# Query projection of a two-layer decoder trunk: sets of 256 columns and all tokens become sets of 512 columns and half of the tokens

## The chip, the core and the metric

The kernel is one program on one core of a Trainium2 chip. A core has five engines with an instruction stream each: TensorE (PE; matrix products from SBUF into the eight PSUM banks, 512 float32 per partition and bank), VectorE (DVE), ScalarE (ACT), GpSimd (POOL), and SyncE (SP), which here only issues DMAs. They run in parallel and meet at semaphores. The metric is the device time of one execution in microseconds (us), the median of several runs.

## What is computed

A gMLP layer with its feed-forward network, keys and values shared by what follows, then an attention layer with its own feed-forward network; 1,024 tokens, width 1,024, everything float32. The change lies in the queries of the attention layer:

```python
def swa_sink_attention(x, k_band, v_band, g_norm, w_q, g_q, sinks, w_o):
    q = (rms_norm(x, g_norm) @ w_q).reshape(b, s, N_Q_HEADS, HEAD_DIM)      # 1024 x 1024 @ 1024 x 1024, 16 heads of 64
    q = rms_norm(q, g_q).reshape(b, nb, BLOCK, N_KV_HEADS, Q_PER_KV, HEAD_DIM)
    logits = jnp.einsum("bntkgd,bnskd->bnkgts", q, k_band)
    ...
```

and just ahead of it, in `shared_kv`, the keys and values: `rms_norm(x, g_kv) @ w_kv` (1,024 x 512), the keys normalised per head as well.

## The kernel before

**Three products for one.** Each float32 operand is split into an upper part (hi, a copy rounded to the type that TensorE reads, made by ScalarE) and the rest (lo, a subtraction by VectorE). `three` issues hi x hi, hi x lo and lo x hi into the same bank.

**Columns.** Between the first feed-forward network and attention, TensorE computes key columns, query columns and value columns. The token tiles (128 tokens; parts `h_hi_b`, `h_lo_b`, one tensor per half of the tokens) are the stationary side, the weights the moving side. `columns(s, ...)` makes one set: 256 output columns for all 8 token tiles, 8 tiles of the inner dimension k, in 4 banks (`4 * s` and up: set 1 writes banks 4 to 7, set 0 banks 0 to 3). First the keys (set 0), then four query sets with s = 1, 0, 1, 0, then the value columns. Sets take turns on the two groups of banks: `cols_free[s]` says that VectorE has read a group, `cols_full[s]` that a set is complete, `cols_half` that the first 4 k are done for all tokens.

**Weights.** A set's weights are two tiles of 128 x 1,024 (4 k x 256 columns each, 512 KB), one for each of two slots. SP loads a tile into `w_raw[slot]` once the tile before it in this slot has been split (`w_ready`), GpSimd multiplies it by the gain of the norm (`gains`, signals `w_scaled`), ScalarE copies the upper part to `w_hi[slot]` (`split_scaled`, signals `w_hi_done`), VectorE subtracts into `w_lo[slot]` (`split`, signals `w_ready`). ScalarE must leave `w_hi[0]` alone until `cols_half`, and `w_hi[1]` until `cols_full`.

**Normalisation.** The token factors come from two matmuls with one column (`mean(2, 0)`, `mean(2, 1)`), which TensorE puts between the key matmuls and which write into banks 6 and 7. VectorE reads each with `mean_square` and signals `rec_done`. Ahead of the first query set TensorE waits for `rec_done` at 6, that is for both. After each set, ScalarE squares the 2,048 elements in PSUM (`head_squares`), VectorE sums them by head, ScalarE takes the root (`head_root`), VectorE refines it and multiplies the set out of PSUM into `q_sb` or `k_sb` (`head_norm`), which frees the banks.

**The order is written out by hand**, engine by engine. TensorE transposes the normalised keys (`keys_first`, into banks 4 and 5) inside the fourth query set, beside entry `(0, 4)`: after 4 k of the fifth token tile. It waits there for the set before to have left banks 4 to 7.

In the code below, `banks` is PSUM, `link` makes VectorE wait for its own last instruction, and `beside` maps a place in a set to something that is issued there.

Of the kernel before, what the change touches and what calls it, by code (L numbers as in the profile page):

```python
# [6 lines left out]
P = 128  # L7
# [3 lines left out]
NCH = T // P  # L11
# [172 lines left out]
def build(nc, x_t, w_av, w_au, w_ao, w_f_in, w_f_out, w_kv, w_q, w_o, w_s, b_s, params, c_dram, x_dram, out_t):  # L184
    ctx = ExitStack()
    with ctx:
        def sem(name):
            return ctx.enter_context(nc.semaphore(name))
# [91 lines left out]
        q_sb = sb("q_sb", [P, NKV, NCH, QPK * HD], F32)  # L280
        k_sb = sb("k_sb", [P, NCH, NKV * HD], F32)
        vv_sb = sb("vv_sb", [P, NCH, NKV * HD], F32)
        kdup = sb("kdup", [P, NCH, 2, HD], F32)
# [24 lines left out]
        dv_lo_first = sb("dv_lo_first", [P, STRIPS, HD], F32R)  # L308
        dv_raw_first = sb("dv_raw_first", [P, STRIPS, HD], F32, plan[0] - 4 * STRIPS * HD)

        def p_of(block):
# [90 lines left out]
        w_ready = [sem(f"w_ready{s}") for s in range(RING)]  # L402
        cols_half = sem("cols_half")
        x_landed = [[sem(f"x_landed{half}_{k}") for k in range(4)] for half in range(2)]
        w_scaled = [sem(f"w_scaled{s}") for s in range(2)]
# [318 lines left out]
        def _(pool):  # L724
# [106 lines left out]
            last.then_inc(consts_done, 1)  # L831
            with pool.Fori(0, 4) as i:
                for c in use:
                    c.enter(i, 1)
                gains(COL_B_NORM)
                for c in use:
                    c.leave(4)
            gains(COL_KV_NORM)
# [103 lines left out]
        def _(act):  # L942
# [73 lines left out]
            for k in (KT - 2, KT - 1):  # L1016
# [3 lines left out]
                                 ACT.Copy).then_inc(ws_hi_done, 1)  # L1020

            def split_pair(s, split):

                act.wait_ge(cols_half, halves.add())
                split(0)
                act.wait_ge(cols_full[s], cols[s].add())
                split(1)

# [347 lines left out]
            def head_root():  # L1376
                act.wait_ge(hms_done, heads.add())
                nc.scalar.activation(small[:, 2, :], small[:, 3, :], ACT.Sqrt).then_inc(hroot, 1)

            act.wait_ge(cols_half, halves.add())  # L1380
            split_scaled(0)
            root(2, 0)
            act.wait_ge(cols_full[0], cols[0].add())
            split_scaled(1)
            root(2, 1)
# [11 lines left out]

            def q_columns(s):
                split_pair(s, split_scaled)
                head_squares(s)  # L1400
                head_root()
# [96 lines left out]

            q_columns(1)
            q_columns(0)  # L1500
            act.wait_ge(cols_free[1], 2 + COLS_A)
            k_twice(0)
            q_upper(0, 0)
            q_columns(1)
            act.wait_ge(consts_done, 8)
            biases(0)
            act.wait_ge(gain_ready, 1)
            keys_upper(4)
            q_columns(0)
            nc.scalar.preload_act_table(ACT.Exp)  # L1510
# [49 lines left out]
        def _(dve):  # L1560
# [585 lines left out]

            def head_norm(s, dst):

                n = heads.add()
                dve.wait_ge(hsq_done, n)  # L2150
                link(nc.vector.tensor_reduce(small[:, 1, :],
                                             nrm[:, 0:2, :].rearrange("p a (h d) -> p (a h) d", d=HD),
                                             AX_X, ALU.add))
                link(nc.vector.tensor_tensor(by_token(small[:, 1, :]), by_token(small[:, 1, :]), r_square, ALU.mult))
                link(nc.vector.tensor_scalar(small[:, 1, :], small[:, 1, :], EPS, None, ALU.add))
                nc.vector.reciprocal(small[:, 3, :], small[:, 1, :]).then_inc(hms_done, 1)
                dve.wait_ge(hroot, n)
                refine(small[:, 2, :], small[:, 2, :], small[:, 1, :], small[:, 3, :])
                link(nc.vector.tensor_tensor(by_token(small[:, 2, :]), by_token(small[:, 2, :]), r_token, ALU.mult))
                nc.vector.tensor_tensor(dst, flat(4 * s, 4).rearrange("p (h d) -> p h d", d=HD),  # L2160
                                        small[:, 2, :].unsqueeze(2).broadcast_to([P, NCH * QPK, HD]),
                                        ALU.mult).then_inc(cols_free[s], 1)
# [5 lines left out]
            r_square = small[:, 0, NCH:2 * NCH].unsqueeze(2).broadcast_to([P, NCH, NKV])  # L2168
            split(0)
            mean_square(2, 0)  # L2170
            token_root(2, 0, 0)
            mean_square(2, 1)
            split(1)
            token_root(2, 1, 0)
# [14 lines left out]

            def q_columns(s, j):  # L2190
                split(0)
                split(1)
                head_norm(s, q_sb[:, j, :, :].rearrange("p n (h d) -> p (n h) d", d=HD))

# [73 lines left out]

            q_columns(1, 0)
            q_columns(0, 1)  # L2270
            q_columns(1, 2)
            keys_lower(4)
            q_columns(0, 3)
            for j in range(NKV):
# [48 lines left out]
        def _(pe):  # L2323
# [485 lines left out]

            columns(1, h_hi_b, h_lo_b)  # L2810
            columns(0, h_hi_b, h_lo_b)
            columns(1, h_hi_b, h_lo_b)
            columns(0, h_hi_b, h_lo_b, None, {(0, 4): keys_first})
            pe.wait_ge(cols_free[1], cols[1].now())
# [92 lines left out]
```

## Time and profile before

| | |
|---|---|
| median of 3 runs | 1923.89 us (1923.83 to 1926.9) |
| the profiled execution | 1924.28 us, its span 1922.6 us |
| TensorE busy | 1899.4 us, 99% |
| VectorE busy | 1455.1 us, 76% |
| ScalarE busy | 890.9 us, 46% |
| GpSimd busy | 471.0 us, 24% |
| bytes by DMA | 199.08 MB, 104 GB/s in the mean |

The span runs from the first to the last instruction of the profiled execution. Matmuls are pipelined, so one row's duration overlaps the next row's; the distance between starts is what a matmul costs. The four query sets lie between 960 and 1053 us. In the answers of the trace, PE is TensorE, DVE VectorE, ACT ScalarE, POOL GpSimd, L with a number is a line of the code above, and x with a number is a count of instructions.

### The profile page before, as it was taken

The page shows a single profiled execution, that of the slowest core. Times are in us where ns is not written, and L with a number is a line of the kernel's source. Part 1 is how long each engine was busy: PE and PEld are TensorE (multiplying, and loading weights), DVE is VectorE, ACT ScalarE, POOL GpSimd, SP SyncE. Part 2 cuts the span into 40 slices and gives each one's busy share as a digit, 9 for nine tenths or more (in the row PEclk, how much of TensorE's full clock was granted, in tenths as well). Part 3 has the DMA queues.
Part 4 walks back from the last instruction along what each step waited for, and adds up shares of the span by engine and source line. Part 5 has one row for each costly group of instructions (what it writes and reads, how often), then busy time and mean ns, then how long its engine had stood idle before and what let it go on. Part 6 is the DMA issues. An engine that isn't in the chain of part 4 may idle for free.

```text
span 1922.6 us, 27830 instructions
## 1 busy us (share of the span) xinstructions
PE 1899.4 (99%) x9784; PEld 1625.6 (85%) x9784; DVE 1455.1 (76%) x2116; ACT 890.9 (46%) x1575; POOL 471.0 (24%) x408
## 2 busy tenths in 40 slices
PE   8999999999999999999999999999999999999999
PEld 8988888878888888888999988878788888888887
DVE  6366758988878876887854677789978887877875
ACT  6242534544444444444522666656444444444443
POOL 0000001333333320011111566651423333301010
PEclk9999999999999999999999999999999999999999
DMA  5111243122212239963111010040222221279681
GB/s 180 45 44 44 88 131 110 66 88 87 87 65 87 87 125 318 294 152 69 34 45 46 11 56 23 12 154 22 100 76 87 87 87 65 97 247 309 180 169 66
DMA packets 63402, 199.08 MB, mean 104 GB/s; under 512 B 5200, under 2 KB 5584, under 8 KB 56144
## 3 DMA queue, kind: packets, MB, share of 16 engines
q1 hardware_dynamic: 48656, 163.29, 24.3%
q0 software_dynamic: 14656, 34.61, 8.3%
q8 instruction: 55, 0.90, 0.2%
q14 instruction: 35, 0.29, 0.0%
HBM read 162.22 MB, written 35.65 MB: 103 GB/s over the span
## 4 chain that ended last, share of the span: by engine, by line
PE 93%; DVE 4%; issue 1%; ACT 1%; DMA 1%; POOL 0%; ACTq 0%; SPq 0%; DVEq 0%
PE banks L2356 29%; PE banks L2358 29%; PE banks L2357 29%; PE banks L2727 2%; DVE xT L1895 1%; PE banks L2705 1%; PE banks L2706 1%; PE banks L2692 1%; DVE xT L1902 1%; PE banks L2753 1%; DVE fw_lo L1853 1%; PE banks L2478 1%; PE banks L2338 0%; DMA b<-c_scratch 0%; DVE xT L1911 0%
## 5 line engine op out<-in xcount | busy, mean ns | idle before, releaser
L2356 PE MATMUL banks<-t_hi,fw_hi 128*128 128x512 f32 x1248 | 487.8, 391 | 5.9 <-issue 1.5
L2358 PE MATMUL banks<-t_hi,fw_lo 128*128 128x512 f32 x1248 | 486.1, 389 | 0.0
L2357 PE MATMUL banks<-t_lo,fw_hi 128*128 128x512 f32 x1216 | 473.6, 389 | 0.0
L2356 PEld LDWEIGHTS banks<-t_hi,fw_hi 128*128 128x128 f32 x1248 | 234.4, 188 | 59.3 <-issue 3.3
L2358 PEld LDWEIGHTS banks<-t_hi,fw_lo 128*128 128x128 f32 x1248 | 234.4, 188 | 48.5
L2357 PEld LDWEIGHTS banks<-t_lo,fw_hi 128*128 128x128 f32 x1216 | 228.4, 188 | 46.8
L752 POOL TENSOR_TENSOR nrm<-raw 128x512 f32<-128x512 f32 x40 | 55.8, 1394 | 721.5 <-DVE fw_lo L1853 428.3
L2356 PE MATMUL banks<-fw_hi,fw_hi 128*128 128x512 f32 x544 | 212.0, 390 | 0.9 <-DVE fw_lo L2012 0.9
L2358 PE MATMUL banks<-fw_hi,fw_lo 128*128 128x512 f32 x544 | 211.9, 389 | 0.0
L2357 PE MATMUL banks<-fw_lo,fw_hi 128*128 128x512 f32 x544 | 211.8, 389 | 0.0
L1299 ACT ACTIVATE fw_hi<-b 128x512 fp32r<-128x512 f32 x154 | 97.1, 631 | 227.0 <-PE banks L2358 215.4
L1214 ACT ACTIVATE xT<-xT,par 128x1024 f32<-128x1024 f32 x88 | 109.3, 1245 | 165.8 <-DVE xT L1881 108.4
L2012 DVE TENSOR_TENSOR fw_lo<-b,fw_hi 128x512 fp32r<-128x512 f32 x154 | 106.4, 691 | 104.7 <-ACT fw_hi L1299 104.6
L1895 DVE SCALAR_TENSOR_TENSOR xT<-xT,par 128x1023 f32<-128x1023 f32 x88 | 150.2, 1707 | 0.0
L1853 DVE TENSOR_TENSOR fw_lo<-raw,fw_hi 128x512 fp32r<-128x512 f32 x120 | 122.4, 1020 | 17.9 <-ACT fw_hi L1188 17.9
L1188 ACT ACTIVATE fw_hi<-nrm 128x512 fp32r<-128x512 f32 x160 | 99.6, 626 | 64.4 <-PE banks L2358 64.4
L1853 DVE TENSOR_TENSOR fw_lo<-nrm,fw_hi 128x512 fp32r<-128x512 f32 x160 | 113.2, 710 | 18.6 <-ACT fw_hi L1188 15.4
L1572 DVE TENSOR_TENSOR w_lo<-w_raw,w_hi 128x1024 fp32r<-128x1024 f32 x43 | 56.8, 1323 | 85.5 <-ACT w_hi L953 43.2
L2356 PEld LDWEIGHTS banks<-fw_hi,fw_hi 128*128 128x128 f32 x544 | 102.2, 188 | 22.7 <-issue 1.8
L2357 PEld LDWEIGHTS banks<-fw_lo,fw_hi 128*128 128x128 f32 x544 | 102.2, 188 | 21.2
L2358 PEld LDWEIGHTS banks<-fw_hi,fw_lo 128*128 128x128 f32 x544 | 102.2, 188 | 21.1
L1902 DVE SCALAR_TENSOR_TENSOR xT<-xT,par 128x1022 f32<-128x1022 f32 x88 | 115.7, 1315 | 0.2
(240 smaller groups left out, 4104.4 us busy)
## 6 DMA issues: line engine op xcount, KB each, us to landing
raw<-in_w_f_in SPq DMA_DIRECT2D x44, 1024.0 KB, 5.0
c_scratch<-xT SPq DMA_DIRECT2D x44, 512.0 KB, 2.6
b<-c_scratch SPq DMA_DIRECT2D x16, 1024.0 KB, 9.5
a_sum<-in_w_f_out POOLq DMA_DIRECT2D x16, 1024.0 KB, 14.5
raw<-in_w_f_out SPq DMA_DIRECT2D x54, 256.0 KB, 11.1
w_raw<-in_w_ao SPq DMA_DIRECT2D x16, 512.0 KB, 3.7
x_scratch<-xT SPq DMA_DIRECT2D x4, 2048.0 KB, 7.9
xT<-x_scratch SPq DMA_DIRECT2D x8, 1024.0 KB, 17.5
```

The costliest lines, as they stand in the source:

```text
L752: nc.gpsimd.tensor_tensor(w_sum(0), a21, a22, ALU.add).then_inc(sums_done, 1)
L1188: nc.scalar.activation(fw_hi[n % RING_F], weight(q, source), ACT.Copy).then_inc(fw_hi_done, 1)
L1214: nc.scalar.activation(y_row(q, r), z_row(q, r), ACT.Identity, bias=par[:, bass.ds(tile + (conv + 6 * FT), 1)], scale=par[:, bass.ds(tile ...
L1299: nc.scalar.activation(tok_hi[n % 3], out_token(n), ACT.Copy).then_inc(c_hi_done, 1)
L1572: nc.vector.tensor_tensor(w_lo[:, slot, :], src[:, slot, :], w_hi[:, slot, :].bitcast(F32), ALU.subtract).then_inc(w_ready[slot], 1)
L1853: nc.vector.tensor_tensor(fw_lo[n % RING_F], weight(q, PRODUCTS[p][0]), fw_hi[n % RING_F].bitcast(F32), ALU.subtract).then_inc(fw_ready, 1)
L1895: link(nc.vector.scalar_tensor_tensor(out=y[:, 1:T], in0=z[:, 0:T - 1], scalar=par[:, bass.ds(i * 2 + (q * FT + r + conv + 2 * FT), 1)], i ...
L1902: nc.vector.scalar_tensor_tensor(out=y[:, 2:T], in0=z[:, 0:T - 2], scalar=par[:, bass.ds(i * 2 + (q * FT + r + conv), 1)], in1=y[:, 2:T], ...
L2012: nc.vector.tensor_tensor(tok_lo[n % 3], out_token(n), tok_hi[n % 3].bitcast(F32), ALU.subtract).then_inc(c_ready, 1)
L2356: nc.tensor.matmul(out, w_h, m_h, start=start, stop=False, **kw)
L2357: nc.tensor.matmul(out, w_h, m_l, start=False, stop=False, **kw)
L2358: return nc.tensor.matmul(out, w_l, m_h, start=False, stop=stop, **kw)
```

## The change

A query set becomes 512 columns for half of the tokens: 4 token tiles, one bank each. `wide_columns(s, pair, half, order, beside)` issues it; the four sets are (columns 0 to 511, first half), (the same columns, second half), and the two for columns 512 to 1,023. The weights of a pair of sets are four pieces of two k x 512 columns (`by_wide` lays them out so), and a piece serves both halves. Four split pieces must stay at hand, so two more places are made, `q_2` over `raw_1` and `q_3` over `vv_sb`, which the values fill later; the raw slots remain two. Pieces 0 and 1 go to `q_2` and `q_3`, pieces 2 and 3 to the old slots 0 and 1, pieces 4 to 7 to slots 0 and 1, `q_2`, `q_3`. `piece_free` counts pieces that a second half is through with. Two heads' groups (j) come out of one set, so the last multiply is two instructions. The value weights' splits go behind `piece_free` 4 and 5.

```diff
+        vv_at = plan[0]
...
+        q_2 = sb("q_2", [P, 2, HB], F32R, raw_1_at)
+        q_3 = sb("q_3", [P, 2, HB], F32R, vv_at)
+        q_slots = [(w_hi[:, 0, :], w_lo[:, 0, :]), (w_hi[:, 1, :], w_lo[:, 1, :]),
+                   (q_2[:, 0, :], q_2[:, 1, :]), (q_3[:, 0, :], q_3[:, 1, :])]
+
+        def q_slot(piece):
+
+            pair, m = piece // 4, piece % 4
+            return q_slots[(m + 2 * (1 - pair)) % 4]
...
-            with pool.Fori(0, 4) as i:
-                for c in use:
-                    c.enter(i, 1)
-                gains(COL_B_NORM)
-                for c in use:
-                    c.leave(4)
+            for piece in range(8):
+                s, k = piece % 2, COL_B_NORM + 2 * (piece % 4)
+                w = w_raw[:, s, :].rearrange("p (k c) -> p k c", k=2)
+                pool.wait_ge(w_landed[s], use[s].add() * 16)
+                nc.gpsimd.tensor_tensor(w, w, par[:, k:k + 2].unsqueeze(2).broadcast_to([P, 2, 512]),
+                                        ALU.mult).then_inc(w_scaled[s], 1)
...
+            def wide_upper(piece):
+
+                slot = piece % 2
+                act.wait_ge(w_scaled[slot], use[slot].add() - LOADS_BEFORE_KV)
+                nc.scalar.activation(q_slot(piece)[0], w_raw[:, slot, :], ACT.Copy).then_inc(w_hi_done[slot], 1)
+
+            wide_upper(0)
+            wide_upper(1)
             act.wait_ge(cols_half, halves.add())
-            split_scaled(0)
+            wide_upper(2)
             root(2, 0)
             act.wait_ge(cols_full[0], cols[0].add())
-            split_scaled(1)
+            wide_upper(3)
             root(2, 1)
             head_squares(0)
             head_root()
...
-            def q_columns(s):
-                split_pair(s, split_scaled)
+            def q_norm(s):
+                act.wait_ge(cols_full[s], cols[s].add())
                 head_squares(s)
                 head_root()
...
-            q_columns(1)
-            q_columns(0)
+            q_norm(1)
+            for piece in (4, 5, 6):
+                act.wait_ge(piece_free, piece - 3)
+                wide_upper(piece)
+            q_norm(0)
+            wide_upper(7)
             act.wait_ge(cols_free[1], 2 + COLS_A)
             k_twice(0)
             q_upper(0, 0)
-            q_columns(1)
+            q_norm(1)
             act.wait_ge(consts_done, 8)
             biases(0)
             act.wait_ge(gain_ready, 1)
             keys_upper(4)
-            q_columns(0)
+            for s in range(2):
+                act.wait_ge(piece_free, 3 + s + 1)
+                split_scaled(s)
+            q_norm(0)
             nc.scalar.preload_act_table(ACT.Exp)
             biases(1)
             q_copy(1, 2)
...
+            def wide_lower(piece):
+
+                slot, (hi, lo) = piece % 2, q_slot(piece)
+                dve.wait_ge(w_hi_done[slot], use[slot].add())
+                nc.vector.tensor_tensor(lo, w_raw[:, slot, :], hi.bitcast(F32), ALU.subtract).then_inc(w_ready[slot], 1)
+
+            wide_lower(0)
             mean_square(2, 0)
+            wide_lower(1)
+            wide_lower(2)
             token_root(2, 0, 0)
             mean_square(2, 1)
-            split(1)
+            wide_lower(3)
             token_root(2, 1, 0)
...
+            def q_norm(s, pair, half):
+
+                n = slice(4 * half, 4 * half + 4)
+                head_factors(lambda row: row.rearrange("p (n h) -> p n h", h=2 * QPK),
+                             *(small[:, 0, t].unsqueeze(2).broadcast_to([P, 4, 2 * QPK])
+                               for t in (slice(NCH + 4 * half, NCH + 4 * half + 4), n)))
+                whole = flat(4 * s, 4).rearrange("p (n j h d) -> p n j h d", n=4, j=2, h=QPK)
+                factor = small[:, 2, :].rearrange("p (n j h) -> p n j h", n=4, j=2)
+                for j in range(2):
+                    last = nc.vector.tensor_tensor(
+                        q_sb[:, 2 * pair + j, n, :].rearrange("p n (h d) -> p n h d", d=HD), whole[:, :, j, :, :],
+                        factor[:, :, j, :].unsqueeze(3).broadcast_to([P, 4, QPK, HD]), ALU.mult)
+                last.then_inc(cols_free[s], 1)
...
-            q_columns(1, 0)
-            q_columns(0, 1)
-            q_columns(1, 2)
+            q_norm(1, 0, 0)
+            for piece in (4, 5, 6):
+                wide_lower(piece)
+            q_norm(0, 0, 1)
+            wide_lower(7)
+            q_norm(1, 1, 0)
             keys_lower(4)
-            q_columns(0, 3)
+            split(0)
+            split(1)
+            q_norm(0, 1, 1)
...
-            columns(1, h_hi_b, h_lo_b)
-            columns(0, h_hi_b, h_lo_b)
-            columns(1, h_hi_b, h_lo_b)
-            columns(0, h_hi_b, h_lo_b, None, {(0, 4): keys_first})
+            def wide_columns(s, pair, half, order, beside=None):
+
+                pe.wait_ge(cols_free[s], cols[s].now())
+                for m in order:
+                    hi, lo = q_slot(4 * pair + m)
+                    if half == 0:
+                        pe.wait_ge(w_ready[m % 2], use[m % 2].add())
+                    for n in range(4):
+                        for k in (2 * m, 2 * m + 1):
+                            c, t = slice(k % 2 * 512, (k % 2 + 1) * 512), slice(n * P, (n + 1) * P)
+                            mm = three(banks[:, 4 * s + n, :], h_hi_b[half][:, k, t], h_lo_b[half][:, k, t],
+                                       hi[:, c], lo[:, c], k == 2 * order[0], k == 2 * order[-1] + 1,
+                                       skip_group_check=True)
+                    if m == order[-1]:
+                        mm.then_inc(cols_full[s], 1)
+                    elif half:
+                        mm.then_inc(piece_free, 1)
+                    if beside is not None and m == order[0]:
+                        beside()
+                cols[s].add()
+
+            wide_columns(1, 0, 0, (0, 1, 2, 3))
+            wide_columns(0, 0, 1, (2, 3, 0, 1))
+            wide_columns(1, 1, 0, (0, 1, 2, 3))
+            wide_columns(0, 1, 1, (0, 1, 2, 3), keys_first)
...
+    def by_wide(w):
+        return w.reshape(4, 2, P, 2, 512).transpose(3, 0, 2, 1, 4).reshape(-1, P, HB)
...
-        "w_q": by_columns(a["b_w_q"][0]),
+        "w_q": by_wide(a["b_w_q"][0]),
```

`head_norm` is cut in two in the change: `head_factors`, which takes the rows of factors as arguments, and the multiply. The hunks stand in this order: tiles, GpSimd, ScalarE, VectorE, TensorE, layout of the weights.

In the built program, VectorE's stretch that begins with the adding up of the squares of norm 2 (`nrm`), before; `small` holds the factors, L1596 with L1598 is a mean's read:

```order
L1589 TENSOR_TENSOR nrm_54<-nrm_54 128x512 [waits sq_added,sq_done] x13
L1572 TENSOR_TENSOR w_lo_61<-w_raw_55,w_hi_60 128x1024 [waits w_hi_done0]
L1596 TENSOR_SCALAR small_53<-banks 128x4 [waits ms_full]
L1598 RECIPROCAL small_53<-small_53 128x4 [waits dve_step]
L1577 TENSOR_TENSOR small_53<-small_53 128x4 [waits root_done]
L1578 SCALAR_TENSOR_TENSOR small_53<-small_53 128x4 [waits dve_step]
L1580 SCALAR_TENSOR_TENSOR small_53<-small_53 128x4 [waits dve_step]
L1596 TENSOR_SCALAR small_53<-banks 128x4 [waits ms_full,dve_step]
L1598 RECIPROCAL small_53<-small_53 128x4 [waits dve_step]
L1572 TENSOR_TENSOR w_lo_61<-w_raw_55,w_hi_60 128x1024 [waits w_hi_done1]
```

The same place in the changed kernel; L2198 is `wide_lower`, L1616 with L1618 a mean's read:

```order
L1609 TENSOR_TENSOR nrm_54<-nrm_54 128x512 [waits sq_added,sq_done] x13
L2198 TENSOR_TENSOR q_2_139<-w_raw_55,q_2_139 128x1024 [waits w_hi_done0]
L1616 TENSOR_SCALAR small_53<-banks 128x4 [waits ms_full]
L1618 RECIPROCAL small_53<-small_53 128x4 [waits dve_step]
L2198 TENSOR_TENSOR q_3_140<-w_raw_55,q_3_140 128x1024 [waits w_hi_done1]
L2198 TENSOR_TENSOR w_lo_61<-w_raw_55,w_hi_60 128x1024 [waits w_hi_done0]
L1597 TENSOR_TENSOR small_53<-small_53 128x4 [waits root_done]
L1598 SCALAR_TENSOR_TENSOR small_53<-small_53 128x4 [waits dve_step]
L1600 SCALAR_TENSOR_TENSOR small_53<-small_53 128x4 [waits dve_step]
L1616 TENSOR_SCALAR small_53<-banks 128x4 [waits ms_full,dve_step]
L1618 RECIPROCAL small_53<-small_53 128x4 [waits dve_step]
```

The second read of a mean stood behind one split and the first token root; it now stands behind three splits and that root, and the third of the three is that of piece 2, the second to wait for `w_hi_done0`.

ScalarE at the same place, before (L953 is a weight split, L966 a root of a token mean):

```order
L953 ACTIVATE w_hi_60<-w_raw_55 128x1024 [waits w_scaled0,cols_half]
L966 ACTIVATE small_53<-small_53 128x4 [waits rec_done]
L953 ACTIVATE w_hi_60<-w_raw_55 128x1024 [waits w_scaled1,cols_full0]
L966 ACTIVATE small_53<-small_53 128x4 [waits rec_done]
L1373 ACTIVATE nrm_54<-banks 128x2048
```

and in the changed kernel (L1389 is `wide_upper`):

```order
L1389 ACTIVATE q_2_139<-w_raw_55 128x1024 [waits w_scaled0]
L1389 ACTIVATE q_3_140<-w_raw_55 128x1024 [waits w_scaled1]
L1389 ACTIVATE w_hi_60<-w_raw_55 128x1024 [waits w_scaled0,cols_half]
L978 ACTIVATE small_53<-small_53 128x4 [waits rec_done]
L1389 ACTIVATE w_hi_60<-w_raw_55 128x1024 [waits w_scaled1,cols_full0]
L978 ACTIVATE small_53<-small_53 128x4 [waits rec_done]
L1378 ACTIVATE nrm_54<-banks 128x2048
```

Two copies came in front of the one that waits for `cols_half`, and that one's tile is now the third of the query weights.

TensorE in the fourth query set, around the key transposes (`kdup`), before, where they follow 108 matmuls of their set:

```order
L2357 MATMUL banks<-w_lo,h_hi_b_106 128x256
L2358 MATMUL banks<-w_hi,h_lo_b_108 128x256
L2774 MATMUL banks<-ident,kdup 128x128 [waits kdup_done,cols_free1,consts_done]
L2774 MATMUL banks<-ident,kdup 128x128 x7
L2356 MATMUL banks<-w_hi,h_hi_b_106 128x256
```

and in the changed kernel, where they follow 24 of 96:

```order
L2404 MATMUL banks<-w_lo,h_hi_b_106 128x512
L2405 MATMUL banks<-w_hi,h_lo_b_108 128x512
L2821 MATMUL banks<-ident,kdup 128x128 [waits kdup_done,cols_free1,consts_done]
L2821 MATMUL banks<-ident,kdup 128x128 x7
L2403 MATMUL banks<-w_hi,h_hi_b_106 128x512
```

The transposes and what they wait for are the same; fewer matmuls, twice as wide, stand in front of them.

## Rows read from the trace of the kernel before

**Rows 1.** The page: span, and each engine's busy time.
```profile
span 1922.6 us, 27830 instructions
...
PE 1899.4 (99%) x9784; PEld 1625.6 (85%) x9784; DVE 1455.1 (76%) x2116; ACT 890.9 (46%) x1575; POOL 471.0 (24%) x408
```

**Rows 2.** The page: chain that ended last, shares by engine.
```profile
PE 93%; DVE 4%; issue 1%; ACT 1%; DMA 1%; POOL 0%; ACTq 0%; SPq 0%; DVEq 0%
```

**Rows 3.** Busy time by window; columns named in the first row.
```profile
core 0: us, PE busy (x) PEld busy (x) DVE busy (x) ACT busy (x) POOL busy (x), PEclk, DMA share, GB/s
...
sum 93.00, PE 93.00 PEld 93.00 DVE 46.76 ACT 20.09 POOL 15.86; mean PE 18.60 PEld 18.60 DVE 9.35 ACT 4.02 POOL 3.17
```

**Rows 4.** Timeline, TensorE, first query set: start us, duration us, what.
```profile
960.11 0.28 PE L2358 MATMUL banks<-w_hi,h_lo_b 128*128 128x256 f32 x1
...
982.91 0.28 PE L2356 MATMUL banks<-w_hi,h_hi_b 128*128 128x256 f32 x1
```

**Rows 5.** Timeline, TensorE, last FFN matmuls, 512 columns.
```profile
923.63 0.39 PE L2358 MATMUL banks<-fw_hi,tail_lo 128*128 128x512 f32 x1
...
935.19 0.39 PE L2358 MATMUL banks<-fw_hi,tail_lo 128*128 128x512 f32 x1
```

**Rows 6.** Timeline, ScalarE: splits (L953), squares (L1373).
```profile
960.43 1.06 ACT L953 ACTIVATE w_hi<-w_raw 128x1024 fp32r<-128x1024 f32 x1 [2.72 <-PE banks L2358]
...
1054.41 1.86 ACT L1373 ACTIVATE nrm<-banks 128x2048 f32<-128x2048 f32 x1
```

**Rows 7.** Timeline, VectorE: splits (L1572), means read (L1596, L1598).
```profile
955.96 1.23 DVE L1572 TENSOR_TENSOR w_lo<-w_raw,w_hi 128x1024 fp32r<-128x1024 f32 x1
...
957.29 0.18 DVE L1598 RECIPROCAL small<-small 128x4 f32<-128x4 f32 x1
...
958.34 0.16 DVE L1596 TENSOR_SCALAR small<-banks 128x4 f32<-128x4 f32 x1
958.53 0.18 DVE L1598 RECIPROCAL small<-small 128x4 f32<-128x4 f32 x1
961.52 2.45 DVE L1572 TENSOR_TENSOR w_lo<-w_raw,w_hi 128x1024 fp32r<-128x1024 f32 x1 [2.81 <-ACT w_hi L953]
963.89 0.15 DVE L1577 TENSOR_TENSOR small<-small 128x4 f32<-128x4 f32 x1
```

**Rows 8.** Timeline, GpSimd: scaling of query weights after their load.
```profile
960.99 1.89 POOL L815 TENSOR_TENSOR w_raw<-w_raw,par 128x1024 f32<-128x1024 f32 x1 [18.43 <-DMA w_raw<-in_w_q]
967.87 1.89 POOL L815 TENSOR_TENSOR w_raw<-w_raw,par 128x1024 f32<-128x1024 f32 x1 [4.99 <-DMA w_raw<-in_w_q]
```

**Rows 9.** Timeline, TensorE, at the program's start.
```profile
6.13 0.55 PE L2356 MATMUL banks<-w_hi,h_hi_a 128*128 128x256 f32 x1 [6.13 <-DVE w_lo L1661]
...
10.53 0.42 PE L2358 MATMUL banks<-w_hi,h_lo_a 128*128 128x256 f32 x1
10.74 0.36 PE L2356 MATMUL banks<-w_hi,h_hi_a 128*128 128x256 f32 x1
```

**Rows 10.** Busy time, granted clock (column PEclk) of two of those microseconds.
```profile
8.00:10.00 2.00, 2.00 (x11) 2.00 (x11) 0.39 (x2) 0.85 (x2) 0.00 (x0) 1.00 0.97 356
```

**Rows 11.** Waits of TensorE: us in total, times, longest us.
```profile
PE banks L2356 <- DVE w_lo L1661: 6.1, 1, 6.1
...
PE banks L2338 <- DVE nrm L1589: 1.0, 1, 1.0
```

**Rows 12.** Timeline, VectorE: last multiply of a normalisation (L2160), values (L2227).
```profile
1038.56 2.29 DVE L2160 TENSOR_TENSOR q_sb<-banks,small 128x2048 f32<-128x2048 f32 x1
...
1060.63 2.29 DVE L2160 TENSOR_TENSOR q_sb<-banks,small 128x2048 f32<-128x2048 f32 x1
...
1068.14 1.22 DVE L2227 TENSOR_TENSOR vv_sb<-banks,small 128x1024 f32<-128x1024 f32 x1
```

**Rows 13.** Timeline, TensorE: key transposes (L2774), query transposes (L2692).
```profile
1042.31 1.04 PE L2774 MATMUL banks<-ident,kdup 128*128 128x128 f32 x8
...
1063.33 0.60 PE L2692 MATMUL banks<-ident,q 128*128 128x128 f32 x4
```

More of the change, by code:

```diff
@@ L403, in build @@
         cols_half = sem("cols_half")
+        piece_free = sem("piece_free")
         x_landed = [[sem(f"x_landed{half}_{k}") for k in range(4)] for half in range(2)]
@@ L1020, in _ @@
                                  ACT.Copy).then_inc(ws_hi_done, 1)
[L1022 to L1026, printed above, removed]
-                split(1)
             def rows_keep(half):
@@ L2145, in _, with head_factors @@
             heads = Count()
-            def head_norm(s, dst):
+            def head_factors(by_token, r_square, r_token):
                 n = heads.add()
@@ L2159, in head_norm @@
                 link(nc.vector.tensor_tensor(by_token(small[:, 2, :]), by_token(small[:, 2, :]), r_token, ALU.mult))
+            def head_norm(s, dst):
+                head_factors(by_token, r_square, r_token)
                 nc.vector.tensor_tensor(dst, flat(4 * s, 4).rearrange("p (h d) -> p h d", d=HD),
@@ L2168, in _ @@
             r_square = small[:, 0, NCH:2 * NCH].unsqueeze(2).broadcast_to([P, NCH, NKV])
-            split(0)
+            def wide_lower(piece):
[3 more added lines that the diff above has]
+            wide_lower(0)
             mean_square(2, 0)
+            wide_lower(1)
+            wide_lower(2)
             token_root(2, 0, 0)
             mean_square(2, 1)
-            split(1)
+            wide_lower(3)
             token_root(2, 1, 0)
@@ L2188, in _ @@
             dve.wait_ge(gain_ready, 1)
[L2190 to L2193, printed above, removed]
+            def q_norm(s, pair, half):
[10 more added lines that the diff above has]
+                last.then_inc(cols_free[s], 1)
             sums = small[:, 7, 0:4]
```

## The prediction

> **What bounds the kernel now.** Read the shares first: TensorE is busy for 1899.4 of 1922.6 us, VectorE for 76% [rows 1], and the chain that ended last is 93% TensorE [rows 2]. So time is saved only where TensorE issues less, and lost wherever it stands. Then read the stretch that the change rewrites, the four sets of query columns: from 960 to 1053 us TensorE is busy for all 93.00 us [rows 3], so each set follows the last without a gap and no wait ends late here. ScalarE, VectorE and GpSimd together have work for less than that, and their waits in this stretch are cover, not cost. That cover is what the change spends.
>
> The unit is the start-to-start pace of TensorE, not the "busy" of a row, which overlaps its neighbours. With 256 columns, 191 matmuls start between 960.11 and 982.91: 22.80 / 190 = 0.1200 us [rows 4]. With 512 columns, 52 start between 923.63 and 935.19: 11.56 / 51 = 0.2267 us [rows 5]. Two narrow ones cost 0.2400, one wide one 0.2267: a matmul has about 13.3 ns that do not depend on its width.
>
> **Part 1, fewer matmuls: -5.1 us.** Each set was 8 tiles of tokens x 8 k x 3 products = 192 narrow matmuls, four sets 768: 768 x 0.1200 = 92.2 us. Now it is 4 tiles x 8 k x 3 = 96 wide ones, four sets 384: 384 x 0.2267 = 87.0 us. All of it is on the path. The Trainium skill (TensorE: Matmul & The Clock Gate, Back-to-back issue gap) gives an isolated matmul its columns over 2.4 GHz plus 2.5 ns; by that the 384 matmuls saved would be worth only 1.0 us, and the sum below would come out 4.1 us higher. This trace has both widths side by side and shows 13.3 ns, so I go by the rows and give that rule no chance of its own.
>
> The bytes, loads, scalings by GpSimd (8 of 1.9 us), splits by ScalarE and VectorE (8 each of 1.06 and about 1.2 us) stay eight each. What moves is their order and what each waits for. The final multiply of a normalisation becomes two of 1,024 elements in place of one of 2,048 (2.29 us [rows 12]). The nearest 1,024-element one took 1.22 us [rows 12], so 2.44 against 2.29: +0.15 us on VectorE, to be counted where somebody waits for it.
>
> **Part 2, the start of the first set: +6.6 us.** TensorE may not open the first query set, which writes banks 4 to 7, before the two token means have been read out of banks 6 and 7 (it waits for rec_done at 6). In the kernel before, the second of these two reads stood behind one split only and ended at 958.71 [rows 7], 1.5 us before the key columns finished: ScalarE's copy, released by their last matmul, starts at 960.43 [rows 6], and a matmul lasts 0.28 us [rows 4] with some 0.05 for the signal, so the last began at 960.1 and the next set at 960.2. The wait was hidden. Now VectorE has wide_lower(1) and wide_lower(2) between the first read and the second, as the rows of the order show. Piece 2 is the third to use raw slot 0 here, and can't be early:
> - wide_lower(0) ends as the old split did, 955.96 + 1.23 = 957.19 [rows 7], and only then may SP load piece 2 into slot 0. GpSimd started on the load that this very moment released at 960.99 and took 1.89 us: scaled at 962.88 [rows 8]. The same here.
> - ScalarE's upper part takes 1.06 us [rows 6]: 963.97.
> - wide_lower(1) follows the first mean's read (957.47) and takes 1.23: 958.7. Its slot's load reaches GpSimd 3.8 to 3.9 us after such a split, as 957.19 to 960.99 and 963.97 to 967.87 [rows 7, 8], so at about 962.6. GpSimd is free at 962.88 and is busy with piece 3 until 964.77.
> - VectorE's subtraction started at 961.52 and took 2.45 us in place of 1.23, ending 1.09 us after GpSimd's end at 962.88 [rows 7, 8]: beside a running GpSimd multiply it makes hardly any way. So wide_lower(2) ends 1.09 us after 964.77, at 965.9, not at 965.2.
> - Three small operations of the root (the first at 963.89, each some 0.2 after the one before) and the two of the mean (958.34 to 958.71, 0.37) [rows 7]: about 0.9 us more. rec_done reaches 6 at 966.75, TensorE starts at 966.8 instead of 960.2: 6.6 us. Without the overlap on VectorE it would be 5.9; both stay in the range.
>
> What is next late after that stall? Piece 3 is ready by 968, and is needed 16 us into the set (3 x 24 x 0.2267). Nothing.
>
> **Part 3, the clock behind that stall: +2.0 us.** Where TensorE stood for 6.1 us, at the program's start [rows 11], its first 21 matmuls of 256 columns, from 6.13 up to the start of the next at 10.74 us, had a pace of some 0.21 us [rows 9], against the 0.12 of [rows 4]. The profile's granted clock reads 1.00 even there [rows 10], but 256 columns in 0.213 us are 1.2 GHz, the lower level. The 21 took 4.61 us where 21 x 0.12 = 2.52 would have done: 2.1 us lost. A stand of 6.4 us (6.6 less the last matmul's run) is as long as that one, and no other wait of TensorE is over 1.0 us [rows 11], so this is the nearest row; I take 2.0 us, with 0 as the other end, since a start from rest need not equal a pause in full work. The same page of the Trainium skill (Why this matters for your kernels) warns against idle gaps between bursts of matmuls for this reason; by it the clock falls here, and denied, the sum is 2.0 us lower.
>
> **Part 4, the key transposes: +3.4 us.** keys_first waits until the set before it has left banks 4 to 7 (cols_free[1]). It stood behind 108 of the fourth set's 192 matmuls, 13.0 us in, and the transposes at 1042.31 [rows 13] came after the normalisation's end (1038.56 + 2.29 = 1040.85 [rows 12]) with 1.4 us to spare. Now it stands behind the first of four pieces: 24 x 0.2267 = 5.4 us in. What it waits for got shorter, but not that short: ScalarE's squares begin some 0.2 us after the set before has issued its last matmul, and from the squares' start at 1054.41 [rows 6] to the end of the last multiply (1060.63 + 2.29 = 1062.92 [rows 12]) are 8.5 us with no GpSimd multiply in it. 0.2 + 8.5 + 0.15 for the second multiply + 0.05 for the signal = 8.9 us; 8.9 - 5.4 = 3.5, and I take 3.4. GpSimd has by then scaled all ten loads, so nothing stretches it. Queued behind this wait on TensorE are the other 72 matmuls of the set and all of the value columns. At the low end, if the squares start at once, it is 3.2.
>
> **What stays covered.** The third set needs piece 7 at 16.3 us. Its raw tile waits for the end of set two, then ScalarE does squares, root and split, VectorE the whole normalisation (8.9 us) and 1.2 us of split: 10 to 11 us. 5 us to spare. Pieces 4 to 6 are released 5.4, 10.9 and 16.3 us into set two; VectorE is through its normalisation at 8.9 us, and the last of the three is split by 16.3 + 1.06 + 1.2 = 18.6 us, before that set ends at 21.8. SP's loads keep their order and their condition (the split of the tile before in the same slot); each waits in its raw slot, scaled, for its release. The value weights are split during the last set (their releases come at its first and second piece, ScalarE passes its key copy about 1 us after the transposes), 8 us before their use. After the last set the query transposes come 84 x 0.12 = 10.1 us in and need a normalisation of 8.9: hidden, as before (1063.33 [rows 13] against 1062.92).
>
> **The sum.** -5.1 + 6.6 + 2.0 + 3.4 = +6.9 us. The profiled execution took 1924.28 us with a span of 1922.6; the median of the three runs is 1923.89, 0.4 below it. I put the sum on the median: 1930.8 us.
>
> **Rivals.**
> - The clock does not fall: -5.1 + 6.6 + 3.4 = +4.9, 1928.8 us. For it: a pause may not be treated as a cold start, and no row shows a clock lost in mid-program. Against: the stand is as long as the one row there is. With the unblocked VectorE it is +4.0, 1927.9.
> - The clock falls in both stands: +9 us, 1932.9. The second stand is half as long as the row that shows it; small.
> - Only one stand occurs, since I have misread one of the two waits. Only the first: -5.1 + 6.6 = +1.5 (or +3.5 with the clock), 1925.4 to 1927.4; only the second: -1.7, 1922.2.
> - Faster: the first stand isn't there because rec_done is not behind piece 2. It would be so if the means' read reached VectorE ahead of wide_lower(2), and the key transposes' wait were over in 5.4 us. Then only the saving stands, 1918.8 us. It decides at the place of one VectorE instruction: the read must be over by 960.2, and piece 2 alone isn't scaled before 962.88. The order speaks against it.
>
> **How the numbers follow.** Forecast 0.62; no clock loss 0.18; one stand only 0.10; no stand 0.07; clock lost twice 0.03. A measurement of this kernel can tell about 0.2% (3.8 us) from no change. Slower by more is the forecast, the double loss and most of the second case (+4.9 is close to the bound: 0.13 of 0.18): 0.78. Within: the rest of it and one stand only, 0.15. Faster: 0.07. The range goes from the unblocked no-clock case with some scatter, 1927.5, to the double loss, 1933.0; outside it lie one stand only, no stand, and a little more: under 2 in 10.
>
> **What would show it.** In the profile after: 384 matmuls of 512 columns with pace 0.227 in this stretch; one TensorE wait of over 6 us released by VectorE's reciprocal of the mean, in front of the first wide matmul; behind it 512-column matmuls at some 0.43 us for about 4 us (part 3), or at 0.227 at once (its rival); one wait of some 3.4 us in front of the eight key transposes. The forecast is wrong if the first wait is under 4 us, if wide matmuls keep another pace, or if a third wait shows up at a set's start.

## The result: 1935.03 us, slower by 10.6 us, and the profile after

| | before | after |
|---|---|---|
| median | 1924.41 us (1923.83 to 1926.9, 5 runs) | 1935.03 us (1934.4 to 1936.73, 5 runs) |
| ratio | | 1.0052, 95% interval 1.004 to 1.0064 |
| span of the profiled execution | 1922.6 us | 1933.3 us |

The way was forecast, the size was not: 1930.8 us was predicted, with a range up to 1933.0. The change is 0.55% of the kernel, small but outside the interval of the ratio. Three of the five runs before are the ones that the forecast was added to.

The page of the changed kernel: span, busy time, and the chain's shares by engine.

```profile
span 1933.3 us, 27052 instructions
...
PE 1900.0 (98%) x9400; PEld 1609.1 (83%) x9400; DVE 1446.7 (75%) x2120; ACT 891.5 (46%) x1575; POOL 473.6 (24%) x408
...
PE 89%; DVE 6%; issue 2%; ACT 1%; DMA 1%; POOL 0%; ACTq 0%; SPq 0%; DVEq 0%
```

TensorE issues 384 matmuls less [rows 1], but its share of the chain falls from 93% [rows 2] to 89%, and VectorE's rises to 6%: TensorE is being waited for less, and waits more. What it waits for stands in the view of its waits (us in total, times, longest us).

```profile
PE banks L2403 <- DVE small L1618: 7.0, 1, 7.0
PE banks L2403 <- DVE w_lo L1681: 6.2, 1, 6.2
PE banks L2821 <- issue: 3.3, 1, 3.3
```

The second row is the old one of the program's start [rows 11]. The first and the third are new, and they are the two stands of the prediction: 7.0 us in front of the first wide set, released by VectorE's reciprocal of a mean (L1618), and 3.3 us in front of the key transposes (L2821), where the view names no releaser ("issue").

The first stand, TensorE's timeline (start us, duration us):

```profile
962.66 0.28 PE L2405 MATMUL banks<-w_hi,h_lo_b 128*128 128x256 f32 x1
969.93 0.80 PE L2403 MATMUL banks<-q,h_hi_b 128*128 128x512 f32 x1 [6.99 <-DVE small L1618]
970.52 0.63 PE L2404 MATMUL banks<-q,h_hi_b 128*128 128x512 f32 x1
970.95 0.63 PE L2405 MATMUL banks<-q,h_lo_b 128*128 128x512 f32 x1
...
973.51 0.63 PE L2405 MATMUL banks<-q,h_lo_b 128*128 128x512 f32 x1
...
974.32 0.39 PE L2404 MATMUL banks<-q,h_hi_b 128*128 128x512 f32 x1
974.55 0.40 PE L2405 MATMUL banks<-q,h_lo_b 128*128 128x512 f32 x1
```

The last key matmul starts at 962.66 and the first wide one at 969.93 in place of 962.78: 7.15 us. Ten wide matmuls start from there up to 974.32: the first two 0.59 us apart, the others 0.43; from 974.32 on it is 0.227, as in [rows 5]. VectorE meanwhile:

```profile
958.52 1.23 DVE L2198 TENSOR_TENSOR q<-w_raw,q 128x1024 fp32r<-128x1024 f32 x1
959.66 0.15 DVE L1616 TENSOR_SCALAR small<-banks 128x4 f32<-128x4 f32 x1
959.85 0.18 DVE L1618 RECIPROCAL small<-small 128x4 f32<-128x4 f32 x1
959.94 1.20 DVE L2198 TENSOR_TENSOR q<-w_raw,q 128x1024 fp32r<-128x1024 f32 x1
966.82 2.18 DVE L2198 TENSOR_TENSOR w_lo<-w_raw,w_hi 128x1024 fp32r<-128x1024 f32 x1 [5.68 <-ACT w_hi L1389]
968.92 0.15 DVE L1597 TENSOR_TENSOR small<-small 128x4 f32<-128x4 f32 x1
...
969.50 0.16 DVE L1616 TENSOR_SCALAR small<-banks 128x4 f32<-128x4 f32 x1
969.70 0.18 DVE L1618 RECIPROCAL small<-small 128x4 f32<-128x4 f32 x1
```

wide_lower(0), the first mean's read, wide_lower(1), then nothing until wide_lower(2) at 966.82, and the second mean's read behind it. In the kernel before, that read followed the first by 1.2 us [rows 7]. GpSimd's two multiplies say what wide_lower(2) waited for and why it took 2.18 us:

```profile
963.74 1.89 POOL L848 TENSOR_TENSOR w_raw<-w_raw,par 128x1024 f32<-128x1024 f32 x1 [18.62 <-DMA w_raw<-in_w_q]
966.02 1.89 POOL L848 TENSOR_TENSOR w_raw<-w_raw,par 128x1024 f32<-128x1024 f32 x1 [0.39 <-DMA w_raw<-in_w_q]
```

Piece 2 is scaled at 965.63; piece 3's multiply runs until 967.91, and wide_lower(2) ends 1.09 us after that, as in [rows 7, 8].

The granted clock (PEclk, third from the end of a row) in windows of 2 us, from 966 on and then from 1042 on:

```profile
core 0: us, PE busy (x) PEld busy (x) DVE busy (x) ACT busy (x) POOL busy (x), PEclk, DMA share, GB/s
966.00:968.00 2.00, 0.00 (x0) 0.00 (x0) 1.18 (x1) 0.88 (x2) 1.89 (x1) 0.86 0.00 0
968.00:970.00 2.00, 0.07 (x1) 0.07 (x1) 1.86 (x7) 1.15 (x2) 0.00 (x0) 0.50 0.00 0
...
972.00:974.00 2.00, 2.00 (x7) 1.54 (x6) 2.00 (x1) 0.00 (x0) 1.10 (x1) 0.50 0.73 190
...
1044.00:1046.00 2.00, 0.00 (x0) 0.00 (x0) 2.00 (x2) 0.03 (x1) 0.00 (x0) 0.99 0.00 0
1046.00:1048.00 2.00, 1.75 (x9) 1.78 (x10) 0.15 (x1) 0.00 (x0) 0.00 (x0) 0.50 0.00 0
1048.00:1050.00 2.00, 2.00 (x7) 1.59 (x7) 0.56 (x1) 1.71 (x2) 0.00 (x0) 0.66 0.00 0
1050.00:1052.00 2.00, 2.00 (x10) 1.66 (x9) 1.86 (x2) 0.35 (x1) 0.00 (x0) 1.00 0.00 0
```

It falls to 0.50 (1.2 of 2.4 GHz) while TensorE stands, both times (the second time just ahead of 1046), and is back at 1.00 some 3 to 4.5 us after work has begun again. The second stand:

```profile
1042.58 0.39 PE L2405 MATMUL banks<-w_hi,h_lo_b 128*128 128x512 f32 x1
1046.25 1.94 PE L2821 MATMUL banks<-ident,kdup 128*128 128x128 f32 x8 [3.29 <-issue]
1047.84 0.78 PE L2403 MATMUL banks<-w_hi,h_hi_b 128*128 128x512 f32 x1
1048.42 0.63 PE L2404 MATMUL banks<-w_lo,h_hi_b 128*128 128x512 f32 x1
```

The eight transposes take 1.6 us there, 0.79 in the kernel before ([rows 13], and the next start at 1043.10), and the wide matmuls behind them start at half pace. The view names no releaser, but the last multiply of the normalisation, in two parts now, ends at 1046.15, 0.10 us before they start:

```profile
1043.80 2.35 DVE L2232 TENSOR_TENSOR q_sb<-banks,small 128x1024 f32<-128x1024 f32 x2
```

They also wait for `kdup`, which ScalarE writes from 1022.0 on, in 1.04 us, so it was there long before.

### The profile page after: what moved, and what is told of

It reads as the page before. It is cut to its first block, busy times and chain, and to the rows that moved or that the text cites. A ratio compares the mean times of both kernels' runs of the same rounds, so it can differ in the third digit from the quotient of the medians.

```text
span 1933.3 us, 27052 instructions
## 1 busy us (share of the span) xinstructions
PE 1900.0 (98%) x9400; PEld 1609.1 (83%) x9400; DVE 1446.7 (75%) x2120; ACT 891.5 (46%) x1575; POOL 473.6 (24%) x408
## 4 chain that ended last, share of the span: by engine, by line
PE 89%; DVE 6%; issue 2%; ACT 1%; DMA 1%; POOL 0%; ACTq 0%; SPq 0%; DVEq 0%
PE banks L2403 28%; PE banks L2405 28%; PE banks L2404 28%; PE banks L2774 2%; DVE xT L1915 1%; DVE xT L1922 1%; PE banks L2752 1%; PE banks L2753 1%; PE banks L2739 1%; PE banks L2800 1%; DMA b<-c_scratch 1%; DVE fw_lo L1873 1%; PE banks L2525 1%; DVE nrm L1609 1%; DVE h_lo_b L2145 0%
## 5 line engine op out<-in xcount | busy, mean ns | idle before, releaser
L770 POOL TENSOR_TENSOR nrm<-nrm,raw 128x512 f32<-128x512 f32 x40 | 83.2, 2079 | 75.3 <-DVE fw_lo L1873 75.3
## 6 DMA issues: line engine op xcount, KB each, us to landing
raw<-in_w_f_out SPq DMA_DIRECT2D x54, 256.0 KB, 10.6
```

Of the source, the lines that this page charges most:

```text
L770: nc.gpsimd.tensor_tensor(w_sum(3), w_sum(1), a12, ALU.add).then_inc(sums_done, 1)
```

## A measure with little scatter

By the traces the changed kernel is 10.7 us longer, but 2.55 us of that arise before the changed code is reached: GpSimd's first instruction there, released by the feed-forward network's last matmul, starts at 938.20 and not at 935.65. So this study compares the stretch from that instruction (the MEMSET of wraps) to ScalarE's first copy of the query transposes (qT), which is the same work in every kernel. Before, and then the changed kernel:

```profile
935.65 0.20 POOL L821 MEMSET wraps<- 128x128 f32 x1 [56.05 <-PE banks L2358]
```

```profile
1063.96 0.60 ACT L1410 ACTIVATE qT<-banks 128x512 fp32r<-128x512 f32 x1 [1.68 <-PE banks L2692]
```

```profile
938.20 0.21 POOL L833 MEMSET wraps<- 128x128 f32 x1 [56.76 <-PE banks L2405]
```

```profile
1075.70 0.60 ACT L1423 ACTIVATE qT<-banks 128x512 fp32r<-128x512 f32 x1 [2.62 <-PE banks L2739]
```

128.31 us against 137.50. The table has this stretch for every profile, and the whole kernel's median less that of the kernel before, as run beside it (for the changed kernel's first row: the five runs above). One profile is one execution, so each stretch is a single reading; the two of the kernel before agree to 0.01 us, the two of the changed kernel to 0.24:

| kernel | stretch, us | less 128.31 | whole kernel, us | interval of the ratio |
|---|---|---|---|---|
| before | 128.31 | | | |
| before, again | 128.31 | 0.00 | -0.4 | 0.9989 to 1.001 |
| changed | 137.50 | +9.19 | +10.6 | 1.004 to 1.0064 |
| changed, again | 137.74 | +9.43 | +10.2 | 1.004 to 1.0067 |
| mean read ahead | 128.34 | +0.03 | +1.5 | 1.0 to 1.0018 |
| keys late | 132.24 | +3.93 | +5.4 | 1.0015 to 1.0038 |
| both | 123.28 | -5.03 | -4.4 | 0.9968 to 0.9986 |
| narrow sets, mean read late | 134.57 | +6.26 | +6.4 | 1.0023 to 1.0045 |
| both, a stand of 2 us made | 125.39 | -2.92 | -2.6 | 0.9979 to 0.9997 |
| both, a stand of 1 us made | 124.03 | -4.28 | -3.7 | 0.9969 to 0.9987 |

## The experiments

**The first stand alone.** One step of VectorE's moved back to where it had been in effect, in the changed kernel:

```diff
             mean_square(2, 0)
+            mean_square(2, 1)
             wide_lower(1)
             wide_lower(2)
             token_root(2, 0, 0)
-            mean_square(2, 1)
             wide_lower(3)
```

> The changed kernel with one VectorE step moved: the read of the second token mean stands right behind the first, ahead of wide_lower(1) and wide_lower(2). Theory (the first stand is the wait for that read, behind piece 2's chain): the stand in front of the first wide set, 7.15 us start to start in the profile after, is gone, and with it the 10 matmuls at half pace behind it (2.1 us); the stand at the key transposes stays. 1935.0 - 9.3 = 1925.7 us. Rival (TensorE would next wait for a piece of weights at the same place): the stand shrinks to the time of that piece, and at least 3 us of the 9.3 stay.

Measured: 1926.78 us (1925.18 to 1929.01, 11 runs) beside 1925.29 of the kernel before (25 runs), 9.1 us less than the +10.6 of the changed kernel. In its trace TensorE has no wait there, and the first wide matmul starts at 962.00, with the next at 962.23:

```profile
962.00 0.40 PE L2403 MATMUL banks<-q,h_hi_b 128*128 128x512 f32 x1
962.23 0.40 PE L2404 MATMUL banks<-q,h_hi_b 128*128 128x512 f32 x1
```

The stretch is 9.16 us shorter. The theory holds (it expected 1.3 us over the kernel before, and 1.5 were measured; the total lies 1 us above the expected 1925.7, as the kernel before lay above its 1924.4); no piece of weights was next late.

**The second stand alone.** In `wide_columns`, in the changed kernel:

```diff
-                    if beside is not None and m == order[0]:
+                    if beside is not None and m == order[1]:
```

> The changed kernel with the key transposes of the fourth wide set behind its second piece (10.9 us in) in place of its first (5.4 us). Theory: the normalisation that they wait for ends 8.9 us in, so the second stand (3.5 us) and the half pace behind it (1.5 us) are gone: 1935.0 - 5.0 = 1930.0 us, with the first stand as it was. Rival (the transposes wait for something else, as the profile names no releaser there): no gain.

Measured: 1930.67 us (1929.23 to 1932.7, 7 runs), 5.4 over the kernel before, so 5.2 less than the changed kernel, where 5.0 were expected; in the stretch 5.26 less. The transposes stand without a wait and take 1.04 us again:

```profile
1048.61 1.04 PE L2821 MATMUL banks<-ident,kdup 128*128 128x128 f32 x8
```

So what they waited for was there 10.9 us into the set, and that it was the normalisation is shown by its end: in the two versions below, in which the wait is shorter, the transposes start 0.10 to 0.11 us after the last multiply once more (1035.77 and 1035.88, 1036.78 and 1036.88).

**Both.**

> Both moves. Theory: no stand is left, only the saving of 384 matmuls: 5.1 us under the kernel before, 1924.4 - 5.1 = 1919.3 us. Rival (the wide form costs something outside the four sets too; the profile after was 2.6 us late already at 936 us, ahead of the changed stretch, and had won back 1.0 us by the end): some 1.5 us of it stays, 1920.9 us.

Measured: 1920.89 us (1919.69 to 1922.55, 11 runs), ratio 0.9977 (0.9968 to 0.9986). This version beats both kernels. In the stretch it gains 5.03 us where 5.1 was the price of part 1. The whole kernel's -4.4 lies between the two expectations (-5.1 and -3.5), and its interval (-6.2 to -2.7 us) holds both. The runs' mean granted clock tells more: 5 of the 11 runs show 1.000, against 17 of 25 of the kernel before, and all others of both 0.999. Among the runs at 1.000 the medians differ by 4.7 us, among those at 0.999 by 5.0. So the missing 0.6 us go with a larger share of runs in which the clock fell somewhere (for the place see "Scatter" below), and the pure saving fits better than its rival. This way of comparing was chosen after the result was seen.

**The same wait with narrow sets**, in the kernel before:

```diff
             split(0)
             mean_square(2, 0)
             token_root(2, 0, 0)
-            mean_square(2, 1)
             split(1)
+            mean_square(2, 1)
```

> The kernel before, narrow sets, with one VectorE step moved: the second mean's read behind split(1). Theory: the same wait as in the changed kernel, with narrow matmuls: split(1) ends at 963.97, the read some 0.3 us later, TensorE starts its first set at 964.4 in place of 960.2: a stand of 4.2 us start to start, and the lower clock behind it for another 1.5 to 2.1: 1924.4 + 6 = 1930.4 us. Rival (the lower clock takes a stand as long as 6 us): 1924.4 + 4.2 = 1928.6 us, and the matmuls behind it at 0.12 us from the first.

Measured: 1931.73 us (1931.07 to 1933.04, 7 runs), +6.4 where +6 was expected. TensorE stands for 3.86 us, and behind that its 256-column matmuls start 0.21 us apart:

```profile
966.90 0.58 PE L2356 MATMUL banks<-w_hi,h_hi_b 128*128 128x256 f32 x1 [3.86 <-DVE small L1598]
967.28 0.42 PE L2357 MATMUL banks<-w_lo,h_hi_b 128*128 128x256 f32 x1
967.50 0.42 PE L2358 MATMUL banks<-w_hi,h_lo_b 128*128 128x256 f32 x1
...
971.34 0.41 PE L2358 MATMUL banks<-w_hi,h_lo_b 128*128 128x256 f32 x1
...
971.91 0.28 PE L2358 MATMUL banks<-w_hi,h_lo_b 128*128 128x256 f32 x1
```

The stand alone is 4.0 us start to start (966.90 in place of 962.88); the other 2.2 of the stretch's 6.26 are the half pace until 971.8. So neither the wide form nor a stand of 6 us is needed for the lower clock: under 4 us do.

**How short a stand is without it.** From the version with both moves, the key transposes put behind one or two token tiles of the second piece (the signals keep their places):

```diff
-                    if beside is not None and m == order[1]:
-                        beside()
+                        if beside is not None and m == order[1] and n == 0:
+                            beside()
```

and `n == 1` in the second.

> As the kernel with both moves, but the key transposes behind the first token tile of the second piece, 6.8 us into the set: a stand of 8.9 - 6.8 = 2.1 us is made, the first stand is absent. Theory A (any stand of some microseconds brings the lower clock): 2.1 + about 1.5 us over the kernel with both moves, 1924.5 us, and a granted clock of 0.5 behind it. Theory B (it takes over 3 us): 2.1 over, 1923.0 us, and a clock of 1.00.

> The same with the transposes behind the second token tile of the second piece, 8.2 us into the set: a stand of 0.7 us. Theory A: 0.7 + up to 1.5 us over the kernel with both moves (1921.6 to 1923.1 us). Theory B: 0.7 over, 1921.6 us, and a granted clock of 1.00 behind it.

Measured: 1923.41 us (1921.99 to 1926.04, 11 runs) and 1922.23 us (1919.94 to 1923.8, 11 runs), beside 1925.97 of the kernel before (27 runs). The waits are 1.92 and 0.56 us in the trace; the version with a wait of 1.92:

```profile
1035.88 1.07 PE L2821 MATMUL banks<-ident,kdup 128*128 128x128 f32 x8 [1.92 <-issue]
```

```profile
1034.00:1036.00 2.00, 0.12 (x1) 0.15 (x2) 1.78 (x2) 0.00 (x0) 0.00 (x0) 1.00 0.00 0
1036.00:1038.00 2.00, 2.00 (x14) 1.78 (x14) 0.00 (x0) 0.96 (x1) 0.00 (x0) 1.00 0.00 0
1038.00:1040.00 2.00, 2.00 (x10) 1.63 (x9) 1.81 (x2) 1.10 (x2) 0.00 (x0) 1.00 0.03 8
```

The clock reads 1.00 throughout, and likewise around the wait of 0.56 us. The stretches are 2.11 and 0.75 us over that of the version with both moves, and that is the stand and nothing more (from 8.9 us: 2.1 and 0.7). That is theory B: here the clock fell behind 3.3 us, and not behind 1.9. One profile each is little, but the mean granted clock of all runs agrees: it is 1.000 in 7 of the 11 runs with the wait of 1.92, about as often as with no wait (5 of 11), and in none of the 11 runs of "mean read ahead", where the wait is 3.3 us (0.997 to 0.999). One of the 11 reads 0.998, so a fall behind 1.92 us now and then isn't excluded.

**Scatter.** The changed kernel and the kernel before once more:

> The changed kernel once more, beside the others of this call. Theory (the 2.6 us by which its first profile was late at 936 us, before the changed stretch, is scatter of this program, from a clock that fell at 38 us in some executions): its time is the kernel before's plus some 9 to 9.5 us, that is -5.1 + 7.15 + 2.1 + 3.5 + 1.5, and not 10.6. Rival (the change costs something in the stretch before it): 10.6 us again.

> The kernel before once more, with a profile. Theory (scatter): the 10 us behind the one wait of 1.0 us at 37 us run at half pace in some executions of it too; if this profile has a granted clock of 0.9 from 30 to 50 us, its span is some 1.7 us over 1922.6. Rival: the clock stays at 1.00 there whenever the sets are narrow and nothing else is moved.

Measured: 1936.19 us (1934.67 to 1937.18, 5 runs), +10.2; and 1925.55 us for the kernel before (8 runs). The window from 36 to 44 us, in which TensorE has a wait of 1.0 us and eight one-column matmuls, in the first profile before, in its second, in the changed kernel and in the version with both moves:

```profile
36.00:44.00 8.00, 6.96 (x58) 6.76 (x58) 4.18 (x12) 5.75 (x12) 0.00 (x0) 1.00 0.23 67
```

```profile
36.00:44.00 8.00, 6.96 (x46) 6.75 (x45) 4.53 (x12) 5.71 (x13) 0.00 (x0) 0.79 0.25 67
```

```profile
36.00:44.00 8.00, 6.96 (x47) 6.76 (x46) 4.35 (x12) 5.71 (x12) 0.00 (x0) 0.79 0.23 67
```

```profile
36.00:44.00 8.00, 6.95 (x59) 6.75 (x58) 4.71 (x12) 5.75 (x12) 0.00 (x0) 1.00 0.22 67
```

In the unchanged kernel, too, the clock is 1.00 there once and 0.79 once, with 58 or 46 matmuls in these 8 us, and it reads 0.79 in 6 of the 10 profiles, of both forms. It costs 1.5 us: from the one-column matmuls at 38 us to the next ones, at 257 us, the first profile before takes 219.02 us and the second 220.52 (37.98 to 257.00, 38.33 to 258.85). Nearly all the rest of the 2.55 us comes at about 745 us, where ScalarE waits for a load from memory, in the first profile before and in the changed kernel's:

```profile
745.92 0.63 ACT L1299 ACTIVATE fw_hi<-b 128x512 fp32r<-128x512 f32 x1 [5.23 <-DMA b<-c_scratch]
```

```profile
748.71 0.63 ACT L1304 ACTIVATE fw_hi<-b 128x512 fp32r<-128x512 f32 x1 [6.33 <-DMA b<-c_scratch]
```

The unchanged kernel's second profile shows both as well (there this wait is 6.24 us), and reaches the changed stretch at 937.84, 2.19 us later than its first. With the 1.5 us taken off where the clock fell, the three narrow profiles reach it between 935.65 and 936.8, the seven wide ones between 935.8 and 937.4. Behind the stretch, from the copy of qT to the end, the narrow ones take 858.46 to 858.60 us, the wide ones 857.56 to 859.08. So no trace shows a cost of wide sets outside the stretch, and one of some 0.5 us isn't excluded.

The median of the changed kernel's second series, +10.2, lies nearer to its rival's 10.6 than to its theory's 9 to 9.5, though its interval (+7.7 to +12.9 us) holds both and its stretch says 9.43. All seven differences of wide kernels lie 0.4 to 1.5 us above their stretch, the narrow ones 0.2 above and 0.4 below. For the version with both moves the share of runs with a mean clock of 0.999 accounts for most of it; for the others it stays open.

## Why the prediction was right or wrong

- **Part 1, -5.1 us: right.** The version without stands measures -5.03 in the stretch, and the wide pace is 0.227. The rule of the Trainium skill for an isolated matmul (TensorE: Matmul & The Clock Gate, Back-to-back issue gap) that I set aside, by which it would have been 1.0 us, doesn't hold for this kernel's streams of matmuls, by the same run.
- **Part 2, +6.6: right, 7.15 and 6.67 us in two profiles.** Cause, place and the overlap on VectorE are as worked out; the first profile has 0.19 us more for piece 2's load (GpSimd starts 3.99 us after the split, not 3.80), and GpSimd's second multiply starts 0.39 us after its first one's end, since piece 3's load landed later than I had put it. Together they are the 0.55 us between 6.6 and 7.15.
- **Part 3, +2.0 behind the first stand: right, 2.1 and 1.6 us.** A set from rest: 24.11 us from its first matmul (969.93) to ScalarE's squares (994.04), against 21.99 in the version without the stand.
- **Part 4, +3.4: right, 3.44 us.** The last matmul ahead of the transposes starts at 1042.58, they start at 1046.25 in place of 1042.81. Keys late took 5.26 us out of the stretch, 1.8 more than that. Nearly all of it is what I left out:
- **The step that failed: part 3 priced one stand only.** I gave the clock's fall behind the second stand a chance of 0.03, because "the second stand is half as long as the row that shows it". The trace before had one stand of 6.1 us and then none above 1.0, so it said nothing on 3.4, and I read the lack of rows as evidence against. It fell in all three profiles with that stand, and cost 1.5 us (changed), 2.8 (changed again: 28.91 us from squares to squares, against 22.69 with no stand and 3.44 of the stand itself) and 1.6 (mean read ahead). The rival "clock falls in both stands" was the true one, in its mechanism: -5.1 + 7.15 + 2.1 + 3.44 + 1.5 = 9.1, against 9.19 in the trace and 6.9 in the forecast. Its number, 1932.9, was still 2.1 us short of the measured median, by 0.55 us of the first stand and by the next point.
- **The base was low.** The median of three runs was 1923.89; of the 25 and 27 runs beside the experiments it is 1925.29 and 1925.97, and the first profile was one of those in which the clock stayed at 1.00 near 38 us. Forecast and range were hung on three runs whose median was low by chance, and that took another 0.5 us beside the runs of the result (1924.41), and up to 2 beside the later ones. Of the 4.2 us between 1930.8 and 1935.03, 2.3 are of the stretch, 0.5 of the base, and 1.4 are the difference between whole kernel and stretch, for which no cause was found.
- The rival "faster" decided at the instruction that I had named, and at the second stand: with the read of the second mean ahead of wide_lower(1) and wide_lower(2) and the transposes 10.9 us in, the same wide sets are faster than the kernel before.
- A slip in the rivals: without the overlap on VectorE the first of them is 4.9 - 0.7 = +4.2, not +4.0.

## What to carry to other kernels

When a rewrite makes one engine's work denser, put every wait of that engine back in terms of time since the set began: the key transposes had stood 13.0 us into their set and now stood 5.4 us in, and a read that had stood behind one split now stood behind three. Price a stand of TensorE twice, its length and the half pace behind it, wherever no row shows that a stand of that length goes free. And compare kernels of a few tenths of a per cent over a stretch between two landmarks, whose length was 128.31 us twice for the kernel before while whole runs scattered by 3.

## What the runs showed that was not expected

- The granted clock fell to 0.50 in stands of 3.3, 3.9 and 6.5 to 7.0 us, stayed at 1.00 behind 1.9 and 0.56, and fell in 6 of 10 profiles behind a wait of 1.0 us with one-column matmuls after it (36 to 44 us). So the length of the wait alone doesn't decide; what else does wasn't tested. The half pace behind a stand cost 1.5 to 2.8 us. The Trainium skill (TensorE: Matmul & The Clock Gate, Why this matters for your kernels) warns against idle gaps between bursts of matmuls. This case agrees, with 1.5 to 2.8 us lost behind each gap of 3.3 us, and nothing behind gaps of 1.9 and 0.56 us.
- In these stands the profile's clock column shows 0.50, while at the program's start it reads 1.00 over the same half pace [rows 9, 10]; there only the distance between starts tells.
